# Feed-forward gate and up units: rounded weights times rounded activations and remainders in one 512-column matmul

## What is computed

```python
def swiglu(h, w_gu, w_out):
    gu = h @ w_gu
    return (jax.nn.silu(gu[..., :FFN_DIM]) * gu[..., FFN_DIM:]) @ w_out

    for i in range(DEPTH_2):        # DEPTH_2 = 4
        ...
        x = x + mix
        x = x + swiglu(rms_norm(x, ffn_norm[i]), f_w_gu[i], f_w_out[i])
```

## Time and profile before

| | |
|---|---|
| median of 3 runs | 2614.94 us (2614.38 to 2615.12) |
| the profiled execution: its own time | 2615.11 us |
| its span, first to last instruction | 2613.3 us |
| PE busy | 2568.4 us, 98% |
| DVE busy | 1441.0 us, 55% |
| ACT busy | 1017.0 us, 39% |
| chain that ended last | PE 96% |

### The profile page before, as it was taken

One profiled execution on the slowest core, in us unless ns is written; L12 is line 12 of the kernel. 1 busy time (PEld: TensorE's weight loads), 2 busy tenths in 40 slices (PEclk: granted clock), 3 DMA queues, 4 the chain that ended last, 5 costly groups with the idle time before them and its releaser, 6 DMA issues.

```text
span 2613.3 us, 51507 instructions
## 1 busy us (share of the span) xinstructions
PE 2568.4 (98%) x20480; PEld 2118.5 (81%) x20480; DVE 1441.0 (55%) x2925; ACT 1017.0 (39%) x1807; POOL 0.2 (0%) x4
## 2 busy tenths in 40 slices
PE   7999999999999999999999999999999999999998
PEld 7997555655565556559999979999999999989998
DVE  6753233323333332348766767667666676677665
ACT  5442111211121112135644556444444544556443
POOL 0000000000000000000000000000000000000000
PEclk9999999999999999999999999999999999999999
DMA  6456999999999999983355433555443345543552
GB/s 267 162 200 266 420 429 429 429 427 429 429 428 428 429 429 428 429 339 130 137 182 181 169 125 119 186 180 178 146 146 130 130 178 179 177 143 124 184 180 93
DMA packets 64350, 665.90 MB, mean 255 GB/s; under 512 B 7136, under 2 KB 7392, under 8 KB 8416
## 3 DMA queue, kind: packets, MB, share of 16 engines
q1 hardware_dynamic: 64224, 664.11, 64.4%
HBM read 663.04 MB, written 1.05 MB: 254 GB/s over the span
## 4 chain that ended last, share of the span: by engine, by line
PE 96%; DVE 2%; ACT 1%; issue 1%; DMA 0%; SPq 0%; DVEq 0%; ACTq 0%
PE bank L2790 18%; PE bank L286 17%; PE bank L287 17%; PE bank L288 17%; PE bank L2808 9%; PE bank L2780 5%; PE bank L2851 2%; PE bank L2797 2%; PE bank L558 1%; PE bank L768 1%; PE bank L788 1%; PE bank L1283 1%; PE bank L2821 0%; PE bank L439 0%; PE bank L429 0%
## 5 line engine op out<-in xcount | busy, mean ns | idle before, releaser
L262 DVE TENSOR_TENSOR w_lo<-ring,w_hi 128x1024 fp32r<-128x1024 f32 (+1 forms) x488 | 575.1, 1217 | 187.1 <-ACT w_hi L255 186.4
L286 PE MATMUL bank<-ht_hi,w_hi 128*128 128x256 f32 x2112 | 606.1, 287 | 0.0
L255 ACT ACTIVATE w_hi<-ring 128x1024 fp32r<-128x1024 f32 (+1 forms) x488 | 488.7, 1046 | 300.6 <-PE bank L288 285.9
L287 PE MATMUL bank<-ht_lo,w_hi 128*128 128x256 f32 x2112 | 598.2, 283 | 0.0
L288 PE MATMUL bank<-ht_hi,w_lo 128*128 128x256 f32 x2112 | 598.1, 283 | 0.0
L286 PEld LDWEIGHTS bank<-ht_hi,w_hi 128*128 128x128 f32 x2112 | 405.8, 192 | 13.9 <-issue 13.1
L287 PEld LDWEIGHTS bank<-ht_lo,w_hi 128*128 128x128 f32 x2112 | 406.0, 192 | 0.8 <-issue 0.7
L288 PEld LDWEIGHTS bank<-ht_hi,w_lo 128*128 128x128 f32 x2112 | 405.8, 192 | 0.0
L2983 DVE TENSOR_SCALAR big<-bank,big 128x64 f32<-128x64 f32 x256 | 61.0, 280 | 328.3 <-PE bank L2797 328.3
L2790 PE MATMUL bank<-ring,big 128*64 128x256 f32 x2048 | 235.1, 382 | 0.1
L2790 PE MATMUL bank<-moe_w,big 128*64 128x256 f32 x2048 | 235.1, 382 | 0.0
(11 more groups left out here) (392 smaller groups left out, 4006.4 us busy)
## 6 DMA issues: line engine op xcount, KB each, us to landing
ring<-post SPq DMA_DIRECT2D x213, 1024.0 KB, 4.8
ring<-wgu SPq DMA_DIRECT2D x64, 2048.0 KB, 14.1
moe_w<-wgu SPq DMA_DIRECT2D x64, 2048.0 KB, 15.8
big<-wdn SPq DMA_DIRECT2D x32, 2048.0 KB, 18.0
moe_w<-wdn SPq DMA_DIRECT2D x32, 2048.0 KB, 16.6
ring<-pre SPq DMA_DIRECT2D x28, 1024.0 KB, 4.8
ring<-post SPq DMA_DIRECT2D x3, 768.0 KB, 4.0
con<-consts SPq DMA_DIRECT2D x1, 1635.5 KB, 14.5
```

The costliest lines, as they stand in the source:

```text
L255: act.activation(w_hi[:, u % SR, cs], ring[:, u % R, cs], ACT.Copy).then_inc(ph.hi, 1)
L262: dve.tensor_tensor(w_lo[:, u % SR, cs], ring[:, u % R, cs], f32(w_hi[:, u % SR, cs]), ALU.subtract).then_inc(ph.lo, 1)
L286: pe.matmul(out, wh, xh, start=start and k == k0, stop=False, **kw)
L287: pe.matmul(out, wh, xl, start=False, stop=False, **kw)
```

## The change

The two products that share the weights `w_hi` become one matmul. `ht_hi` and `ht_lo` become the two halves of one tensor `both`, which lies where they lay, and a matmul reads 256 columns of each half, 512 in all. Columns 0 to 255 of the bank collect `w_hi*ht_hi + w_lo*ht_hi`, and columns 256 to 511 collect `w_hi*ht_lo`. Gate and up so take a whole bank each, and a gate-up unit takes a pair of banks (`bank_pair`). The two halves have to be added afterwards: ACT copies the low halves of both banks to SBUF (`lows`, 128x512), DVE adds the high halves to them (`pre_act`, 128x512), and only then scales the gate. `lows` waits for PE's unit; the addition waits for `lows`. PE waits before gate-up q for the addition of q-2. This holds for q = 1 to 21 of each layer; gate-up 0 stays as it was. ACT and DVE also take their work in another order: the two halves of rounding, and of subtracting, of unit u+2 no longer stand together.

```diff
@@ -151,8 +151,8 @@
         xt = sb("xt", [P, KB, S])
 
         ht_at = -(-nc.sbuf_base // 32) * 32
-        ht = sb("ht_hi", [P, KB, S], F32R)
-        hl = sb("ht_lo", [P, KB, S], F32R)
+        both = sb("ht", [P, 2, KB, S], F32R)
+        ht, hl = both[:, 0, :, :], both[:, 1, :, :]
         hid_hi = sb("hid_hi", [P, 4, S], F32R)
         hid_lo = sb("hid_lo", [P, 4, S], F32R)
         w_hi = sb("w_hi", [P, SR, UW], F32R)
@@ -177,7 +177,9 @@
         small = sb("small", [P, 64])
         items = sb("items", [1, 1 + 2 * ITEMS], I32)
         UNIT = UW * 4
-        bank = [ctx.enter_context(nc.psum_tensor(f"bank{b}", [P, 512], F32)) for b in range(8)]
+        bank = [ctx.enter_context(nc.psum_tensor(f"bank{b}", [P, 512], F32)) for b in range(4)]
+        bank_pair = [ctx.enter_context(nc.psum_tensor(f"bank_pair{b}", [P, 2, 512], F32)) for b in range(2)]
+        bank += [bank_pair[b // 2][:, b % 2, :] for b in range(4)]
 
         def c(name):
             a, n = CONST[name]
@@ -222,6 +224,7 @@
         s_fpq, s_fpe, s_fy, s_fyc = sem("fft_seq_done"), sem("fft_seq_copied"), sem("fft_group_done"), sem("fft_out_copied")
         s_sc, s_max, s_exp, s_prob, s_tr, s_pt, s_pv, s_o = (sem("att_" + n) for n in ("scores", "max", "exp", "prob", "turned", "probt", "pv", "out"))
         s_sig = sem("ffn_sigmoid")
+        s_low, s_fu = sem("ffn_low_copied"), sem("ffn_banks_read")
         s_out = sem("out_written")
 
         block = ctx.enter_context(nc.Block())
@@ -1960,6 +1963,8 @@
         full = area(8, 2).rearrange("p (b n) -> p b n", n=S)
         gup = area(10, 2).rearrange("p (b n) -> p b n", n=S)
         sr2 = area(12, 2).rearrange("p (b n) -> p b n", n=S)
+        low = area(14, 4).rearrange("p (b g n) -> p b g n", b=2, n=S)
+        pre_act = area(18, 4).rearrange("p (b g n) -> p b g n", b=2, n=S)
         sig_count = [0]
 
         def ffn_stage(l, hand, gain, eps):
@@ -2006,6 +2011,34 @@
                         mm.then_inc(s_fb, 1)
                 mm.then_inc(post_done, 1)
 
+            def pair_of(q):
+                return bank_pair[(t0 % 4 // 2 + q) % 2]
+
+            def place(h):
+
+                return (t0 + 1 + h) % 2
+
+            def wide_unit(pe, u, q, i):
+
+                wait_unit(pe, POST_PH, u, i, UP, part=0)
+                if q < 3:
+                    pe.wait_ge(s_evac, t0)
+                else:
+                    pe.wait_ge(s_fu, g0 + q - 1 + i * TP)
+                wh, wl = (w_[:, u % SR, :].rearrange("p (k n) -> p k n", k=KB) for w_ in (w_hi, w_lo))
+                for h in range(2):
+                    if h and q == 1:
+                        hand.total(pe)
+                    if h and q == 2:
+                        pe.wait_ge(s_fu, g0 + 1)
+                    o, cs = pair_of(q)[:, place(h), :], slice(h * P, (h + 1) * P)
+                    for k in range(KB):
+                        if k == KB // 2 and h == 0:
+                            wait_unit(pe, POST_PH, u, i, UP)
+                        pe.matmul(o, wh[:, k, cs], both[:, :, k, :], start=(k == 0), stop=False, skip_group_check=True)
+                        mm = pe.matmul(o[:, 0:S], wl[:, k, cs], ht[:, k, :], start=False, stop=(k == KB - 1), skip_group_check=True)
+                mm.then_inc(post_done, 1)
+
             def step_pe(pe, j, i=0):
                 for u, q, o in in_order(j):
                     if o is not None:
@@ -2013,7 +2046,7 @@
                     elif q == 0:
                         project_first(pe, POST_PH, u, t0, "T", hts, hand)
                     else:
-                        project(pe, POST_PH, u, t0 + q, "T", hts, KB, i, UP, TP, between=hand.total if q == 1 else None)
+                        wide_unit(pe, u, q, i)
 
             def each(eng, step):
                 for j in (0, 1):
@@ -2027,6 +2060,12 @@
                 each(pe, step_pe)
                 out_unit(pe, FB // 2 - 1)
 
+            def lows(act, q, i):
+                act.wait_ge(post_done, gu(q) + 1 + i * UP)
+                if q >= 3:
+                    act.wait_ge(s_fu, g0 + q - 1 + i * TP)
+                act.activation(low[:, q % 2, :, :], pair_of(q)[:, :, S:2 * S], ACT.Copy).then_inc(s_low, 1)
+
             def sigmoid(act, q, i):
                 act.wait_ge(s_fg, g0 + q + 1 + i * TP)
                 if g0 + q >= 2:
@@ -2043,18 +2082,23 @@
                 if j == 0:
                     split_act(act, POST_PH, gu(0) + SR)
                     hand.root(act)
-                    split_act(act, POST_PH, gu(1) + SR)
-                    for q in (0, 1):
-                        sigmoid(act, q, i)
+                    round_part(act, POST_PH, gu(1) + SR, 0)
+                    sigmoid(act, 0, i)
+                    lows(act, 1, i)
+                    round_part(act, POST_PH, gu(1) + SR, 1)
+                    sigmoid(act, 1, i)
                     for q in (0, 1):
                         round_hidden(act, q, i)
                     return
                 for u, q, o in in_order(j):
-                    if o is None:
-                        sigmoid(act, q, i)
-                    split_act(act, POST_PH, u + SR, i, UP)
-                    if o is None:
-                        round_hidden(act, q, i)
+                    if o is not None:
+                        split_act(act, POST_PH, u + SR, i, UP)
+                        continue
+                    lows(act, q, i)
+                    round_part(act, POST_PH, u + SR, 0, i, UP)
+                    sigmoid(act, q, i)
+                    round_part(act, POST_PH, u + SR, 1, i, UP)
+                    round_hidden(act, q, i)
 
             def act_(act):
                 each(act, step_act)
@@ -2070,10 +2114,18 @@
                 dve.wait_ge(post_done, gu(q) + 1 + i * UP)
                 if g0 + q >= 2:
                     dve.wait_ge(s_sig, g0 + q - 1 + i * TP)
-                tb = tile_bank(t0 + q)
-                dve.tensor_tensor(gsc[:, q % 2, :], tb[:, 0:S], rows, ALU.mult).then_inc(s_fg, 1)
+                if q == 0:
+                    tb = tile_bank(t0)
+                    dve.tensor_tensor(gsc[:, 0, :], tb[:, 0:S], rows, ALU.mult).then_inc(s_fg, 1)
+                    dve.wait_ge(s_fg, g0 + 1)
+                    dve.tensor_tensor(gup[:, 0, :], gsc[:, 0, :], tb[:, S:2 * S], ALU.mult).then_inc(s_fu, 1)
+                    return
+                dve.wait_ge(s_low, l * (FB - 1) + q + i * TP)
+                dve.tensor_tensor(pre_act[:, q % 2, :, :], pair_of(q)[:, :, 0:S], low[:, q % 2, :, :], ALU.add).then_inc(s_fu, 1)
+                dve.wait_ge(s_fu, g0 + q + 1 + i * TP)
+                dve.tensor_tensor(gsc[:, q % 2, :], pre_act[:, q % 2, place(0), :], rows, ALU.mult).then_inc(s_fg, 1)
                 dve.wait_ge(s_fg, g0 + q + 1 + i * TP)
-                dve.tensor_tensor(gup[:, q % 2, :], gsc[:, q % 2, :], tb[:, S:2 * S], ALU.mult)
+                dve.tensor_tensor(gup[:, q % 2, :], gsc[:, q % 2, :], pre_act[:, q % 2, place(1), :], ALU.mult)
 
             def hidden(dve, q, i, base):
                 k = base + q + i * TP
@@ -2107,7 +2159,10 @@
                     if o is None:
                         scale_gate(dve, q, i)
                         split_hidden(dve, q - 1, i, base[0])
+                        split_part(dve, POST_PH, u + SR, 0, i, UP)
                         hidden(dve, q, i, base[0])
+                        split_part(dve, POST_PH, u + SR, 1, i, UP)
+                        continue
                     elif o == FB // 2 - 2:
                         split_hidden(dve, FB - 1, i, base[0])
                         break
```

## The result

| | before | after |
|---|---|---|
| median of 20 runs each | 2614.84 us (2611.47 to 2617.32) | 2618.93 us (2618.09 to 2621.55) |
| ratio, 95% interval | | 1.0017 (1.0011 to 1.0024) |
| profiled execution, its span | 2613.3 us | 2618.9 us |
| a feed-forward stage, from the matmuls of one norm sum (L507, now L510) to the next (three stages) | 191.17, 191.25, 191.16 us | 191.78, 191.89, 191.82 us |

What follows compares the result with a forecast made beforehand. PE, busy in 764.2 of 765.1 us of the feed-forward stages, was taken as the bound. Saving 7.7 us on matmuls and adding 10.1 us of waits at stage ends gave +2.4 us: 2617.4 us, range 2608 to 2628.

Steps and rivals of the forecast that it cites:

- PE's triple: Gate-up units 1 to 21: one 512- and one 256-column matmul take 354.3 ns instead of 360, saving 7.7 us.
- My own sign of being wrong: Prediction called wrong if the pair of matmuls isn't additive, or waits at a stage's start are much longer or absent.
- Wait ahead of unit 3: Start of each stage: PE waits 0.6 us for DVE's late subtraction, 0.7 us with the first weight load.
- Wait ahead of unit 4: Start of each stage, output 0: PE waits 1.05 us for part 0's subtraction, 1.15 us with the load.
- Wait ahead of output 10: End of each stage: PE waits 0.5 us for `hid_lo` of q = 21, 0.6 us with the load.
- the 0.3 us that I added for the second stage: Second stage's start: an existing PE wait eats gate-up 1's gain, so waits count 10.1 us instead of 9.8.
- No wait in the loop: Gate-up units in the loop: weights of unit u+2 are ready with slack of 1.7 and 1.2 us.
- ACT and DVE: All 84 wide units: copies add 50 us on ACT, additions 57 us on DVE.
- The sum: Whole kernel: -7.7 us on PE plus 10.1 us of waits gives +2.4 us, 2617.4 us.
- the wide matmul saves nothing: Rival for the gate-up units: a 512-column matmul costs 240 ns, time 2625.0 us; chance 0.25.
- A new wait in every unit of the loop: Rival: part 1 comes after U+7.09 in 64 loop units, 6.4 us per 0.1 us beyond, 2624 us; chance 0.08.
- weight loads bound PE: Rival for the gate-up units: one load in three removed, triple 351.4 ns, 2613.4 us or 2608.4; chance 0.17.

Runs made afterwards that it cites:

- no_fold: The changed kernel without ACT's copy and DVE's addition, wide matmuls kept, old ACT and DVE order, part of the result missing: 2603.38 us, ratio 0.9962 against before.
- grouped: The changed kernel with two 512-column matmuls followed by two 256-column ones instead of alternating: 2611.54 us, ratio 0.9986 against before.

## Why the prediction was right

2617.4 us were predicted and 2618.93 measured, inside 2608 to 2628 and within 0.2% of before. By its steps:

- **PE's triple.** 354.3 ns forecast, 352.75 measured (353.5 with the boundaries between units). The term was taken too small: 1344 x 7.25 = 9.7 us, or 9.5 with the boundaries, not 7.7; `no_fold`, in which nothing waits, gives 9.8. In the loop the sum of the earlier trace rows is off by 1 ns only (353.3, a wide one at 234); what I had not seen is the faster pace of gate-up 1 and 2, nearly 8 ns below the sum of the two prices. My own sign of being wrong, a pair that isn't additive, holds there, and in `grouped`.
- **Wait ahead of unit 3.** 0.7 forecast, the first load behind it included; 0.90 measured and 0.10 behind the first matmul, 1.0 in all (0.8 of it still there with narrow matmuls). Counted from the start of ACT's rounding, DVE's subtraction came at 1312.74 - 1307.84 = 4.90 us where I had 4.74, and PE was done with unit 2 at 1313.12 - 1307.84 = 5.28 where I had 5.41, since that unit has the faster pace.
- **Wait ahead of unit 4.** 1.15 forecast, 1.12 and 0.10 measured.
- **Wait ahead of output 10.** 0.6 forecast, 0.67 and 0.07 measured. In all 12.0 us, not 10.1. Of the 10.1, the 0.3 us that I added for the second stage have no row behind them: half a unit gains 0.05 us by my own price, and the stretch ahead of that norm sum takes 112.28 us, 112.24 before.
- **No wait in the loop.** Right in all four stages.
- **ACT and DVE.** +50 and +57 us busy forecast, +58 and +58 measured. DVE's additions take 58.1 us, ACT's copies 50.1. ACT's other 8 are in the rounding, 497.3 us now and 488.7 before: its two parts no longer stand together, where two took 2.01 us for twice 1.05.
- **The sum.** By the measured terms -9.5 + 12.0 = +2.5 us; the three stages that were measured whole, with the fourth like them, give +2.55. I had -7.7 + 10.1 = +2.4. That this fits so well is luck: gain and waits were each taken about a fifth too small, and the errors cancel. The runs give +4.1. What is left, 1.5 us, lies outside the stages, where I had predicted nothing. Both profiles of the change have a place of that size, the clock's fall behind a wait of 1.75 us. That it is this in the median run, and that the change brings it about, is not shown.
- **The chances.** Those for slower add up to 0.37, not 0.36.

The rivals: that the wide matmul saves nothing is excluded by `no_fold` against before. A new wait in every unit of the loop did not come. That weight loads bound PE would have given 351.4 ns or less. The loop's 353.3 is above that, but 346.5 in gate-up 2 and 348.3 in `grouped` are below it, so 354.3 isn't a floor. Whether the loads have to do with it isn't shown: the number of loads is the same at either pace. The Trainium skill (Perfetto Trace Analysis, section Identifying the Most-Contended Engine) would have the busy share of the loads, beside the arithmetic done, as the measure of how close TensorE is to its limit: here a third fewer loads in these units took that share from 100% to 90% of a stage and gave 2% on the triple. The trace bears it out only that far. Its formula for the gap between matmuls (TensorE: Matmul & The Clock Gate, section Back-to-back issue gap) gives, by my estimate, 325.0 ns for a wide and a narrow one; no pair here comes under 346. The section gives that formula for a matmul by itself and not for a stream with a load before each, so it was not the right one for my comparison.

The signs were right for the reasons given, and the experiments show both terms apart. That they nearly cancel was an accident of the order on ACT: with two calls on ACT moved, the four stages go from +2.5 us to -6.9, and the runs from +4 to -9, a part of that with the clock.

## What to carry to other kernels

When PE is the bound and busy all the time, a gain on PE is small but sure, and what decides is whether the added work on other engines delays the first and the last unit of a stage, where no unit lies between producer and consumer. Look there for a table load or a slow instruction standing ahead of the new link, and put the new link first. Where only one or two units of a loop lose, leave them as they were.

## What was not expected of the hardware

- An fp32r matmul of 512 columns with one of 256 behind it takes 353.3 ns in most units and 346.5 in some, at the same granted clock of 1.00; one program had either in the same unit in two executions. Order of the two doesn't matter (353.5), groups of two take 348.3, groups of eight 349.2. The cause is open.
- A small fp32 matmul of 2 columns between two fp32r units costs some 0.2 us (4.0 us per stage for 21, in which the waits are 0.6 us shorter), more than the 0.12 of an fp32r matmul of 256 columns.
- Behind a wait of PE the first matmul is followed 0.07 to 0.10 us later than others are, which the idle time does not show (338 ns for 235, 221 for 120).
- Behind a wait of PE of 1.75 us the granted clock fell to half in some profiles (15 matmuls at 213 ns for 120, 1.5 us lost) and not in others, with the same code. Such stretches, here and at other places outside the stages, make up most of the spread of a kernel: two profiles of one program differ by 8.1 us, 7.0 of them in three stretches between the norm sums in which the mean clock differs.
